# Issuing the feed-forward transposition trips from GpSimd instead of SyncE

## The reference, cut to what matters

```
first model, per layer   (D_FF = 4096)
    m = rmsnorm(h, norm_mlp_pre[i])
    m = square(relu(m @ w_up[i]))
    m = m @ w_down[i]
    h = h + rmsnorm(m, norm_mlp_post[i])

second model, twice per layer   (D_FF_2 = 2816)
    gate, up = split(u @ w_in)
    h = (silu(gate) * up) @ w_out
    x = x + 0.5 * rmsnorm_2(h, post_g)
```

## Time and profile before

| | us |
|---|---|
| median of 3 runs | 2295.41 (2295.13 to 2295.47) |
| the profiled execution's own time | 2296.12 |
| its span, first to last instruction | 2294.1 |
| TensorE busy (matmuls) | 2272.3 |
| TensorE weight loads, beside the matmuls | 1906.5 |
| DVE busy | 1524.4 |
| ScalarE busy | 1176.3 |
| GpSimd busy | 79.4 |

### The profile page before, as it was taken

How to read it: one execution, slowest core, us unless ns; L and a number is a source line. 1 busy time by engine, 2 the same in 40 slices (tenths; PEclk the granted TensorE clock), 3 DMA queues, 4 the chain that set the end, 5 groups by cost and what they waited for, 6 DMA issues and landing times.

```text
span 2294.1 us, 28606 instructions
## 1 busy us (share of the span) xinstructions
PE 2272.3 (99%) x11228; PEld 1906.5 (83%) x11228; DVE 1524.4 (66%) x1955; ACT 1176.3 (51%) x1650; POOL 79.4 (3%) x134
## 2 busy tenths in 40 slices
PE   8999999999999999999999999999999999999998
PEld 6888888888888888988888888888889888888887
DVE  6876657776666567886575665665578865756654
ACT  6554546464455446756443544444467563444542
POOL 0110000100000000000000000000000000000000
PEclk9999999999999999999999999999999999999999
DMA  8447856457747655657665576576546576555762
GB/s 337 147 139 269 290 179 213 147 195 273 267 165 266 239 185 161 210 190 231 222 200 189 162 270 233 192 272 242 181 161 213 187 230 226 190 198 165 257 229 101
DMA packets 152916, 483.02 MB, mean 211 GB/s; under 512 B 17232, under 2 KB 40016, under 8 KB 152528
## 3 DMA queue, kind: packets, MB, share of 16 engines
q1 hardware_dynamic: 152784, 481.21, 61.9%
HBM read 455.98 MB, written 25.17 MB: 210 GB/s over the span
## 4 chain that ended last, share of the span: by engine, by line
PE 92%; DVE 5%; ACT 1%; issue 1%; POOL 0%; DMA 0%; DVEq 0%; POOLq 0%; ACTq 0%
PE ub L1781 17%; PE ub L1783 17%; PE ub L1782 17%; PE acc L1781 9%; PE acc L1783 8%; PE acc L1782 8%; PE ub L1813 5%; PE ub L1810 3%; PE ub L1788 1%; DVE wlo L1098 1%; PE ub L1789 1%; PE ub L1790 1%; PE acc L1844 1%; DVE work L1301 1%; PE acc L2251 0%
## 5 line engine op out<-in xcount | busy, mean ns | idle before, releaser
L1098 DVE TENSOR_TENSOR wlo<-raw,whi 128x1024 fp32r<-128x1024 f32 x776 | 911.4, 1218 | 368.4 <-ACT whi L600 367.0
L600 ACT ACTIVATE whi<-raw 128x1024 fp32r<-128x1024 f32 x776 | 780.1, 1053 | 481.6 <-PE ub L1783 296.8
L1781 PE MATMUL ub<-whi,xhl 128*128 128x512 f32 (+1 forms) x1472 | 573.7, 390 | 3.7 <-DVE wlo L1098 1.3
L1783 PE MATMUL ub<-whi,xhl 128*128 128x512 f32 (+1 forms) x1472 | 571.2, 388 | 0.0
L1782 PE MATMUL ub<-wlo,xhl 128*128 128x512 f32 (+1 forms) x1472 | 571.2, 388 | 0.0
L1781 PEld LDWEIGHTS ub<-whi,xhl 128*128 128x128 f32 x1472 | 276.8, 188 | 62.5 <-DVE wlo L1098 2.0
L1783 PEld LDWEIGHTS ub<-whi,xhl 128*128 128x128 f32 x1472 | 276.9, 188 | 56.7
L1782 PEld LDWEIGHTS ub<-wlo,xhl 128*128 128x128 f32 x1472 | 277.0, 188 | 55.1
L1781 PE MATMUL acc<-whi,bhl 128*128 128x512 f32 x736 | 288.0, 391 | 0.0
L1783 PE MATMUL acc<-whi,bhl 128*128 128x512 f32 x736 | 286.6, 389 | 0.0
L1782 PE MATMUL acc<-wlo,bhl 128*128 128x512 f32 x736 | 286.4, 389 | 0.0
(11 more groups left out here) (299 smaller groups left out, 2273.4 us busy)
## 6 DMA issues: line engine op xcount, KB each, us to landing
raw<-in_w SPq DMA_DIRECT2D x776, 512.0 KB, 5.4
turns<-FB SPq DMA_DIRECT2D x24, 512.0 KB, 3.0
FB<-turns SPq DMA_DIRECT2D x96, 128.0 KB, 2.9
gain<-in_gains SPq DMA_DIRECT2D x20, 512.0 KB, 7.9
tapw<-in_taps SPq DMA_DIRECT2D x16, 512.0 KB, 4.0
turns<-tS SPq DMA_DIRECT2D x8, 512.0 KB, 6.1
tS<-turns SPq DMA_DIRECT2D x32, 128.0 KB, 3.0
turns<-PB SPq DMA_DIRECT2D x8, 512.0 KB, 7.3
```

Of the source, the lines that this page charges most:

```text
L600: do(act.activation(whi[:, s % RING, c], raw[:, slot, c], ACT.Copy), counts["w_hi"])
L1098: do(dve.tensor_tensor(wlo[:, s % RING, c], raw[:, PLACES[s][0], c], whi[:, s % RING, c].bitcast(f32), ALU.subtract), counts["w_lo"])
L1781: pe.matmul(o, x_h, w_h, start=first, stop=False, skip_group_check=True)
L1783: return pe.matmul(o, x_l, w_h, start=False, stop=last, skip_group_check=True)
```

## The change

The 38 feed-forward trips move from SyncE's program into GpSimd's. SyncE keeps the eight trips of the retention heads; their rows in `turns` come behind those of the feed-forward blocks. In GpSimd's program a block's trips stand one behind the other, ahead of the block's `post` roots: each waits for the next `blocked`, issues the put, waits for its landing and issues four gets. The semaphore `sent` counts puts that landed; `back0` and `back1` take the place of `moved0` and `moved1` for these gets, on which ScalarE waits. The DMAs move the same bytes in the same pieces.

```diff
+        FFN_TRIPS = len(ENDS1) * LAYERS + 2 * len(ENDS2) * LAYERS
...
-                    sp.dma_start(turned_rows[g * P:(g + 1) * P, 0:src.shape[1]], src).then_inc(sem["put"], 16)
+                    sp.dma_start(turned_rows[(FFN_TRIPS + g) * P:(FFN_TRIPS + g + 1) * P, 0:src.shape[1]], src).then_inc(sem["put"], 16)
...
-                        for end, b in ENDS1.items():
-                            if s == s1(L, "ffn", end + 7 if b else end + 6):
-                                put("blocked", area1(b))
-                                get(area1(b))
...
-                        for name in ("f1", "f2"):
-                            for end, b in ENDS2.items():
-                                if s == s2(L, name + "first", end + 7 if b else end + 6):
-                                    put("blocked", area2(b))
-                                    get(area2(b))
...
+                def trip(area, g):
+
+                    n = area.shape[1] // 4
+                    nxt("blocked")
+                    pool.dma_start(turned_rows[g * P:(g + 1) * P, 0:4 * n], area).then_inc(sem["sent"], 16)
+                    pool.wait_ge(sem["sent"], 16 * (g + 1))
+                    for c in range(4):
+                        pool.dma_start(area[32 * c:32 * c + 32, :].rearrange("j (a x) -> j a x", a=4),
+                                       turned_rows[g * P:(g + 1) * P, c * n:(c + 1) * n].rearrange("(a j) x -> j a x", a=4)
+                                       ).then_inc(sem[f"back{g % 2}"], 16)
...
                     for t in range(2):
                         post(t)
                         pre(t)
+                    for i, b in enumerate(ENDS1.values()):
+                        trip(area1(b), ffn1_trip(L, i))
                     for t in range(2):
                         post(t)
...
+                    for i, b in enumerate(ENDS2.values()):
+                        trip(area2(b), ffn2_trip(L, 0, i))
                     for t in range(2):
                         post(t, 4 * EPS)
                         pre(t)
...
+                    for i, b in enumerate(ENDS2.values()):
+                        trip(area2(b), ffn2_trip(L, 1, i))
                     for t in range(2):
                         post(t, 4 * EPS)
...
-                    nxt(f"moved{arrivals[0] % 2}", 64)
-                    arrivals[0] += 1
+                    nxt(f"{name}{arrivals[name] % 2}", 64)
+                    arrivals[name] += 1
...
-                    moved()
+                    moved("back")
```

More of the change, by code:

```diff
@@ L289, in build @@
                  "root_ready coef_ready has xs sd md sigs exd va vah oq ro sm2 pv2 rp rph rx sc2 mh mx mixed par_free "
-                 "va_done fa fg fp fr blocked pb put moved0 moved1").split()
+                 "va_done fa fg fp fr blocked pb put moved0 moved1 sent back0 back1").split()
         sem = {n: ctx.enter_context(nc.semaphore(n)) for n in names}
@@ L343, in acc_bank, with ffn1_trip, ffn2_trip @@
             return 2 * t + fb
+        FFN_TRIPS = len(ENDS1) * LAYERS + 2 * len(ENDS2) * LAYERS
+        def ffn1_trip(L, i):
+            return len(ENDS1) * L + i
+        def ffn2_trip(L, f, i):
+            return len(ENDS1) * LAYERS + len(ENDS2) * (2 * L + f) + i
         def waiter(eng):
@@ L384, in get @@
                         sp.dma_start(dst[32 * c:32 * c + 32, :].rearrange("j (a x) -> j a x", a=4),
-                                     turned_rows[g * P:(g + 1) * P, c * n:(c + 1) * n].rearrange("(a j) x -> j a x", a=4)
+                                     turned_rows[(FFN_TRIPS + g) * P:(FFN_TRIPS + g + 1) * P, c * n:(c + 1) * n].rearrange("(a j) x -> j a x", a=4)
                                      ).then_inc(sem[f"moved{g % 2}"], 16)
@@ L642, in sines_by_token, with moved @@
                     do(act.activation(cc[:, :, 8:16], yc, ACT.Sin), counts["sin_ready"])
-                arrivals = [0]
-                def moved():
-                    nxt(f"moved{arrivals[0] % 2}", 64)
-                    arrivals[0] += 1
+                arrivals = Counter()
+                def moved(name):
+                    nxt(f"{name}{arrivals[name] % 2}", 64)
+                    arrivals[name] += 1
                 def turned_hi(u0, area, blocks_=1, q=4):
-                    moved()
+                    moved("back")
                     for t in range(2):
@@ L974, in turned_p @@
                     def turned_p(hd):
-                        moved()
+                        moved("moved")
                         for t in range(2):
```

## The result

The changed kernel takes 2308.26 us in the median of six runs (2306.88 to 2317.61), against 2295.3 us for the kernel before (2295.13 to 2295.47, six runs). The ratio is 1.0061 with an interval of 1.0051 to 1.0072: slower by 0.6%, 13 us, and above the stated range of 2293.5 to 2303.

A forecast was written before the change was run, and what follows sets the result against it. TensorE, busy 99% of the span, was taken to bound the kernel; gain 0, other trips 0 and a 0.2 us layer 1 stall gave 2295.6 us on the 2295.41 median, range 2293.5 to 2303.

The forecast's parts named there:

- What bounds the kernel: All six feed-forward stretches: TensorE is busy for the whole window, so trips are wholly hidden.
- the gain of nothing: SyncE no longer waiting for turned blocks and landing puts: gain 0, since TensorE does not see those waits.
- The faster rival: Freed SyncE brings weights earlier and remaining TensorE gaps close, at most 7.6 us: 2290 us; chance 0.04.
- The place and the margins: First trip of each first-model feed-forward, before its down projection: margin 4.5 us in layer 0, 4.2 in layer 1.
- The price of an issue: Each GpSimd DMA, five per trip: 1.09 us, between 0.33 and 2.57, so a trip grows by 3.4 us.
- The dear-DMA rival: First trips stall because a GpSimd DMA issue costs more, 1.83 us: 2300.8 us, 2329 at 2.57; chance 0.11.
- one more term eats at that rest: SyncE's loads overlapping the first trips' gets: 1 us taken, at most 2.6; layer 0 keeps 0.1, layer 1 stalls 0.2.
- The other 36 trips have more room: Trips other than the two first ones: their down projections come many chunks later and ScalarE is held; cost 0.
- GpSimd shut out by DVE: DVE's run of remainders holds the first put 6.8 us in each first-model layer: 11.7 us, 2307.1 us; chance 0.10.
- The roots: Square roots on GpSimd, queued behind the trips, with DVE's residual waiting for them: cost 0.

The follow-up runs named there:

- the last experiment: Changed kernel, but the first and last trip of each first-model feed-forward back on SyncE, the other 34 on GpSimd: 2295.45 us, ratio 1.0 to the kernel before.
- the first experiment: Changed kernel, but only the first trip of each first-model feed-forward back on SyncE, the other 36 on GpSimd: 2297.78 us, ratio 1.0015 to the kernel before.
- third experiments: Changed kernel, but SyncE holds its loads at the first trip's old place until the four gets have landed: 2306.9 us, ratio 1.0052 to the kernel before.

## Why the prediction was wrong, point by point

**What bounds the kernel, and the gain of nothing: right.** TensorE paced every stretch, and a freed SyncE could give it nothing. SyncE's waits for these puts are gone, and its waits for free weight places grew from 1410 to 1815 us. The faster rival fell with the last experiment: 34 trips moved, ratio 1.0. One reading was wrong: 6.76 us is not ScalarE's longest wait for a trip in the kernel before, as its waits (us in total, times, longest) show:

```profile
ACT bhl L657 <- DMA FB<-turns: 28.4, 5, 8.9
```

TensorE's windows are full all the same, so the conclusion holds.

**The place and the margins: right.** The first trip of each first-model block is where growth meets TensorE. Landing had to come by 182.5 in layer 0; it came at 186.32, 3.8 late, and TensorE lost 3.73. In layer 1 all stood 6 us later by then (put 505.53 instead of 499.15, GpSimd's extra 0.3 aside), so the limit was about 520.9; the copies began at 523.94, 3.0 late, and TensorE lost 3.0.

**The price of an issue: too high, and not what decided.** I took 1.09 us, from an add over 128 rows. The line's instructions (ns, min/median/max) show half of that:

```profile
L523 POOL DMA_DIRECT2D FB<-turns x120: 548/551/581, 173.2 to 2269.0; - x120
L520 POOL DMA_DIRECT2D turns<-FB x30: 558/561/782, 167.2 to 2263.1; - x30
```

Five issues of the first trip took 0.78 + 2.21 = 2.99 us, 0.9 more than SyncE's 2.08, not 3.4. With this price and the loads held nothing is lost (2295.64 us, all trips on GpSimd). The dear-DMA rival had the right place and the wrong cause.

**The step that failed: "one more term eats at that rest".** I put the loads' effect on the gets at 1 us and bounded it at 2.6, as 5.2 us of head start shared by two streams. It measured 11.0 - 5.7 = 5.3 us on the gets, and the put's landing grew too (167.22 + 0.78 to 173.15 is 5.2 us, against 3.5). The first copies start 8.3 us later than before (186.32 against 178.00): 5.3 from the gets, 1.7 from the put's landing, 0.9 from the issues and 0.5 from a later start; the forecast had 4.4 in all. Two things were wrong in the step. I counted the head start, and the experiment with the loads held until the put shows that cutting it brings nothing: what counts is that the gets lost their turn ahead of the loads. And I held the loads back to 173.5 by the wait for a weight place, but SyncE's gains went out at 169.57.

**Left out: the clock.** In the changed kernel each of the two gaps is followed by a stretch at a lower granted clock that costs 1.7 us. It is no fixed price: with only the first trips on GpSimd it was 2.9 us behind one gap and nothing behind the other.

**"The other 36 trips have more room": wrong for one of seven in the first model.** I judged each trip by itself. But ScalarE's late copy of one block delays the next block's columns, so the trips fall behind one after the other, until the copy of the last stands ahead of the last splits (first and third experiments). In the first experiment TensorE lost nothing before it in layer 0, and yet the last block was turned at 282.2 us instead of 276.2, and copied at 298.1 instead of 285.6.

**GpSimd shut out by DVE: fell.** The first put was issued at 167.22 and took 0.78 us, inside DVE's run of remainders from 166.83 to 173.69, and no get took over 0.581 us. This rival's 2307.1 us comes nearest to the measured 2308.26, by luck: the put was not held. The Trainium skill's "SBUF — State Buffer", Who interferes with whom, has it that a DVE tensor_tensor with both inputs in SBUF contends with GpSimd's reads; nothing in this trace speaks against it.

**The roots: right.** GpSimd's first operation of a root took 363 and 709 ns in the mean, against 368 and 772 before; the norms did not move.

## What to carry to other kernels

A queue is an order as well as an issuer. Before a small urgent transfer is moved out of a queue of bulk loads, ask what stood behind it there: in a queue of its own it shares the engines with all of that, by packets, and here took twice as long. Judge a wait that an idle engine absorbs by the tightest consumer, and follow the lateness from block to block; and count with a gap on TensorE the slow clock that may follow it.

## What was not expected of the hardware

The turns by packet show in the counts (227 to 229, 237 to 232, 324 to 333), whichever engines issue. The same gets make packets of 3.3 KB on the average from GpSimd and 1.8 KB from ScalarE, and the smaller ones fare worse. The full engines also move fewer bytes while gets are under way: 265 GB/s from 178 to 184 us in the changed kernel. The second queue is not needed for that, as the kernel before shows (windows, columns as in the earlier trace rows), where the gets had landed by 178.00:

```profile
172.00:178.00 6.00, 6.00 (x28) 4.98 (x27) 3.90 (x6) 2.99 (x5) 0.00 (x0) 1.00 1.01 244
178.00:184.00 6.00, 6.00 (x28) 4.97 (x27) 6.00 (x9) 4.20 (x6) 0.00 (x0) 1.00 1.02 414
```

It moved 244 GB/s while the gets ran in the loads' own queue, and 414 after. Why was not tried. Nor was it tried why single runs of the changed kernel reach 2317.61 us; the mean granted clock of that run is 0.996, against 0.998 of most.
